# A transformer block in three-term fp32r: the two feed-forward stages start by token halves, with eight plain products in place of the first seven combined ones

## The reference, cut to what matters

```python
x = x + 0.5 * swiglu(rmsnorm(x, ffn1_norm), ffn1_w_gate, ffn1_w_up, ffn1_w_down)   # D_FF = 2816
h = rmsnorm(x, mix_norm)                                  # attention and RWKV-7 mixing on h @ w_in
...
x = x + merged @ w_out
x = x + memory_cross_attention(rmsnorm(x, cross_norm), rmsnorm(mem, mem_norm), w_cq, w_ckv, w_co)
x = x + 0.5 * swiglu(rmsnorm(x, ffn2_norm), ffn2_w_gate, ffn2_w_up, ffn2_w_down)
out = rmsnorm(x, final_norm)
# rmsnorm(x, g) = x * rsqrt(mean(x * x) + 1e-6) * g;  swiglu(h) = (silu(h @ gate) * (h @ up)) @ down
```

## Time and profile before

| | us |
|---|---|
| median of 3 runs (3218.71 to 3220.97) | 3220.22 |
| the profiled execution, its own time | 3219.02 |
| its span in the trace | 3217.2 |
| TensorE busy in it (91%) | 2943.0 |
| VectorE, GpSimd, ScalarE busy | 1621.0, 1353.7, 1087.4 |

### The profile page before, as it was taken

The page is one execution under the profiler, slowest core; times in us unless marked ns, Lnnn a source line. Parts: engine busy times, 40 slices in busy tenths (PEclk is TensorE's granted clock), DMA queues, the critical chain, the costliest instruction groups (busy, mean ns, idle before and its releaser), DMA issues. The chain is left out here.

```text
span 3217.2 us, 61692 instructions
## 1 busy us (share of the span) xinstructions
PE 2943.0 (91%) x26984; PEld 2412.2 (75%) x26984; DVE 1621.0 (50%) x1767; ACT 1087.4 (34%) x1780; POOL 1353.7 (42%) x705
## 2 busy tenths in 40 slices
PE   3799999996899999999999998899995799999995
PEld 2688888885677878778787887686774688887885
DVE  5654443445146666555666665243224645543445
ACT  2433333223234434334443333342212333333221
POOL 1344444443255555444555454462131344444441
PEclk7999999998999999999999999899997899999997
DMA  3222224442421211131121212351002222234441
GB/s 143 69 94 96 83 105 147 144 147 49 175 62 51 59 58 58 37 108 47 46 61 53 63 43 74 116 160 46 26 27 79 69 79 85 98 109 145 143 147 69
DMA packets 260169, 279.12 MB, mean 87 GB/s; under 512 B 13504, under 2 KB 213312, under 8 KB 257728
## 3 DMA queue, kind: packets, MB, share of 16 engines
q1 hardware_dynamic: 259904, 275.20, 26.2%
HBM read 224.83 MB, written 50.33 MB: 86 GB/s over the span
## 5 line engine op out<-in xcount | busy, mean ns | idle before, releaser
L483 POOL TENSOR_TENSOR w_low<-ffn_work,w_high 128x1024 fp32r<-128x1024 f32 x182 | 444.9, 2445 | 668.7 <-ACT w_high L556 395.4
L523 PE MATMUL bank<-h_high,w_high 128*128 128x512 f32 x1232 | 484.8, 393 | 59.1 <-DVE h_low L667 34.9
L523 PE MATMUL bank<-h_low,w_high 128*128 128x512 f32 x1232 | 483.4, 392 | 0.0
L523 PE MATMUL bank<-h_high,w_low 128*128 128x512 f32 x1232 | 483.4, 392 | 0.0
L1228 POOL TENSOR_TENSOR mix_panel_low<-arena,mix_panel_high 128x1024 fp32r<-128x1024 f32 x114 | 276.3, 2425 | 406.2 <-ACT mix_panel_high L1605 406.2
L1334 PE MATMUL bank<-mix_h_high,mix_panel_high 128*128 128x512 f32 (+1 forms) x896 | 357.7, 399 | 21.1 <-POOL mix_panel_low L1228 16.0
L1334 PE MATMUL bank<-mix_h_low,mix_panel_high 128*128 128x512 f32 (+1 forms) x896 | 342.0, 382 | 0.0
L1334 PE MATMUL bank<-mix_h_high,mix_panel_low 128*128 128x512 f32 (+1 forms) x896 | 340.7, 380 | 0.0
L714 DVE TENSOR_TENSOR h_low<-ffn_work,h_high 128x512 fp32r<-128x512 f32 x88 | 204.4, 2323 | 250.4 <-ACT h_high L571 250.4
L523 PEld LDWEIGHTS bank<-h_high,w_high 128*128 128x128 f32 x1232 | 234.1, 190 | 112.2 <-issue 61.4
L540 PE MATMUL bank<-h_high,w_high 128*128 128x512 f32 x704 | 274.8, 390 | 4.4 <-DVE h_low L714 4.4
(11 more groups left out here) (276 smaller groups left out, 5784.4 us busy)
## 6 DMA issues: line engine op xcount, KB each, us to landing
arena<-w_in SPq DMA_DIRECT2D x96, 512.0 KB, 3.8
ffn_work<-w_down SPq DMA_DIRECT2D x88, 512.0 KB, 3.6
a_spill<-ffn_work SPq DMA_DIRECT2D x88, 256.0 KB, 2.2
ffn_work<-a_spill SPq DMA_DIRECT2D x88, 256.0 KB, 2.6
ffn_work<-w_gate SPq DMA_DIRECT2D x12, 1024.0 KB, 5.7
ffn_work<-w_up SPq DMA_DIRECT2D x12, 1024.0 KB, 8.2
arena<-w_gate SPq DMA_DIRECT2D x10, 1024.0 KB, 5.6
arena<-w_up SPq DMA_DIRECT2D x10, 1024.0 KB, 8.2
```

The costliest lines, as they stand in the source:

```text
L483: nc.gpsimd.tensor_tensor(slot(w[1], q), src, slot(w[0], q).bitcast(F32), ALU.subtract).then_inc(s_low, 1)
L523: last = mm(bank[:, bk, :], w[wp][:, q % RING, kt, e], h[hp][:, k, kt], start=fresh and kt + wp + hp == 0, stop=kt == KT // 2 - 1 and wp = ...
```

## The change

Three parts go together.

**Start of the first feed-forward.** The block that loaded x is gone. x comes in 8 tiles of 128 tokens (`load_rows`), through three row buffers; ScalarE squares each tile in its buffer and sums the squares on the way (`accum_out`), TensorE turns it, VectorE (tiles 0 to 3) or ScalarE (4 to 7) puts it into `xT`. The norm runs over 512 tokens at a time.

**First group of both feed-forwards.** Eight plain products (`FIRST`) with five panels (`FIRST_PANELS`, one of them twice), those of token half 0 first; T1 to T4 are used from group 1 on.

**End of cross attention.** The closing projection makes panels 0 and 1 for both halves, then 2 to 7 for half 0, then 2 to 7 again for half 1, each with its own load, high and low part. The norm of half 0 for `ffn(1)` is made in between, its first weights are loaded and its first panel is split there. In `project_out` all low parts of panels go to VectorE; in the closing projection those of the first six units go to VectorE and the rest to GpSimd.

```diff
+        FIRST_PANELS = [A11, A12, A21, A22, A11]
+        FIRST = [(0, B11, C11, True), (1, B21, C11, False), (2, B11, C21, True), (3, B21, C21, False),
+                 (1, B22, C12, True), (3, B22, C22, True), (2, B12, C22, False), (4, B12, C12, False)]
```

SyncE in `ffn(0)` (`load_rows`; `keep_x(j)` waits until 256 tokens are placed and stores them, 1 MB), then in both:

```diff
+                        def tile(t):
+                            if t >= 3:
+                                sp.wait_ge(s_sq, t - 2)
+                            sp.dma_start(tiles[t % 3], d["x"][t * P:(t + 1) * P, :]).then_inc(s_tile[t % 3], 16)
...
+                        for t in range(3):
+                            tile(t)
+                        sp.dma_start(par[:], ...).then_inc(s_par, 16)
+                        first_weights(0)
+                        tile(3)
+                        keep_x(0)
+                        tile(4)
+                        keep_x(1)
+                        for t in range(5, 8):
+                            tile(t)
+                        first_weights(1)
+                        sp.dma_start(cst[:, n:], d["consts"][:, n:]).then_inc(s_rest, 16)
...
+                    keep_act(0, 0)
+                    keep_act(0, 2)
+                    sp.wait_ge(s_blow, low_at["T2"])
+                    sp.wait_ge(s_bsum, sums_before["T2"])
                     load_group(1)
```

GpSimd:

```diff
+                        nrm[0].pool_root(pool)
+                        subtract_low(0, block_of(0, FIRST_PANELS[0]))
...
+                    for q in range(1, NQ0):
+                        subtract_low(q, block_of(0, FIRST_PANELS[q]))
+                        if front and q == 1:
+                            nrm[1].pool_root(pool)
```

TensorE:

```diff
+                    if front:
+                        pe.wait_ge(s_ident, 16)
+                        for t in range(4):
+                            turn_tile(t)
+                        nrm[0].pe_scale(pe)
+                    else:
+                        nrm[1].pe_sums(pe)
+                    for r in range(len(FIRST)):
+                        first_product(r)
+                        if front and r < 2:
+                            turn_tile(4 + 2 * r)
+                            turn_tile(5 + 2 * r)
+                        elif front and r == 2:
+                            nrm[1].pe_scale(pe)
```

ScalarE:

```diff
+                    if front:
+                        for t in range(4):
+                            square_tile(t)
+                        round_first(0)
+                        nrm[0].act_high(act, range(0, 2))
+                        round_first(1)
+                        nrm[0].act_high(act, range(2, 6))
+                        place_tile(4)
+                        nrm[0].act_high(act, range(6, 8))
+                        place_tile(5)
+                        square_tile(4)
+                        square_tile(5)
+                        round_first(2)
+                        for t in (6, 7):
+                            place_tile(t)
+                        for t in (6, 7):
+                            square_tile(t)
+                    else:
+                        round_first(1)
+                        round_first(2)
+                    round_input("B22")
+                    round_first(3)
+                    round_input("B12")
+                    first_silu(0)
+                    round_input("T1")
+                    first_silu(2)
+                    round_input("T3")
+                    round_first(4)
+                    round_input("T2")
```

VectorE, behind the norm of half 1 with the scaling and low parts of B22 and B12:

```diff
+                    input_sum("T1", half_of(0, 0), half_of(0, 1), half_of(0, 0))
+                    input_sum("T3", half_of(0, 1), half_of(1, 1), half_of(0, 1))
+                    first_multiply(0)
+                    input_lows("T1")
+                    first_multiply(2)
+                    input_lows("T3")
+                    input_sum("T2", half_of(1, 1), half_of(1, 1), half_of(0, 0))
+                    input_lows("T2")
```

`cross`, SyncE (`keep_x` stores 1 MB each, once the given number of sums is there):

```diff
-                    for k in range(CO, CO + KT):
+                    for k in range(CO, CO + 4):
                         load(sp, k)
+                    sp.wait_ge(s_o, 2 * XH)
+                    for e, w in enumerate((panels(d["w_gate2"]), panels(d["w_up2"]))):
+                        sp.dma_start(ffn_raw[:, :, e], w[:, :, 0:2 * P]).then_inc(s_ffn, 16)
+                    for k in range(CO + 4, CO + KT + 2):
+                        load(sp, k)
+                    keep_x(0, 0, 10)
+                    keep_x(0, 1, 10)
+                    for k in range(CO + KT + 2, FFN_PANEL):
+                        load(sp, k)
+                    keep_x(1, 0, 12)
+                    keep_x(1, 1, 16)
```

`cross`, TensorE (`CLOSE` is 14):

```diff
+                    for u in range(2, CLOSE):
+                        panel_ready(pe, CO + u)
...
+                        out_part(u, 0, KT).then_inc(s_ready, 1)
+                        if u == KT:
+                            nf[0].pe_sums(pe)
+                        elif u == KT + 1:
+                            nf[0].pe_scale(pe)
```

`cross`, VectorE in `project_out`:

```diff
                         add_out(dve, n, o, k % 4, k + 1)
+                        subtract_low(dve, k % 2, k + 2, V)
```

783 lines of the change are left out of this document (458 added, 325 removed).

## The result

The changed kernel takes **3142.54 us** (median of 4 runs, 3142.12 to 3144.54) against 3220.59 before: a ratio of 0.976, 95% interval [0.975, 0.977], so 78 us less. Its profiled execution took 3142.14 us with a span of 3140.4, against 3219.02 and 3217.2 before: 76.9 us less. I had forecast 3143.

What follows compares the result with a forecast made beforehand. TensorE was 91% busy, its idle time mainly at both feed-forward starts, with group 0 bound by VectorE. Gains of 25.1 + 52 + 1 = 78.1 us took 3219.0 to 3140.9, median forecast 3143; 8 in 10: 3128 to 3162.

Steps and rivals of the forecast that it cites:

- First border: Start of first feed-forward up to group 1: group 1 starts at 103.5 instead of 128.6, 25.1 us gained; bounds 17 to 39.
- the 2 us that I charged VectorE: Price assumed in the forecast: VectorE loses 2 us for each panel low part that GpSimd makes beside it.
- the 112 that I gave: Sign in the first feed-forward: group 1's first addition at 112, from a start at 103.5 plus 8.2.
- The store of x: First border: scaling waits until 512 tokens of x are stored, at 21; 15.5 by the Trainium skill's rate.
- Squares with a sum on the way: Price of ScalarE's squaring with summing in the row tiles: taken as 1.1 us, at least 1.06, at most twice that.
- project_out: Low parts moved to VectorE fit its load and GpSimd's source low parts come earlier: 1 us gained; bounds -2 and +4.
- Closing projection and second border: Closing projection ends at 2445 against 2444.2; second feed-forward's group 1 starts at 2494 against 2547.6: 52 us gained, bounds 44 to 55.
- (a): Rival, first border: order of instructions does not bind; group 1 at 90 to 95, 10 us more gained, 3132; chance 0.13.
- (b): Rival, both groups 0: VectorE stays the bound, group 1 starts 8 later at each border, 3159; chance 0.13.
- (c): Rival, closing projection: stalls repeat in every unit, 12 units at 7.3 instead of 5.44, 22 us lost, 3165; chance 0.08.
- (d): Rival, groups after the borders: they lose their rhythm; gain gone at 3.9 us a group, 3243 at 5; chance 0.04.
- (e): Rival, both borders: nothing gained, idle time only moves behind the first products; 3218 to 3222; chance 0.02.

Runs made afterwards that it cites:

- e1: Changed kernel with, in the first border, ScalarE making panel 3's high part before the four of B22, not behind them; 3148.21 us, ratio 0.9766.
- e2: Changed kernel with, in the first border, GpSimd making panel 2's low part before the second half's root; 3137.52 us, ratio 0.9736.
- e3: Changed kernel with first border reordered: second half of first weights before tile 7, panels 2 and 3 split earlier, before the second root; 3133.04 us, ratio 0.9725.
- e8: Changed kernel with TensorE turning all eight row tiles before product 0 in the first border; 3142.44 us, ratio 0.9754.
- e6: Changed kernel with project_out's panel low parts back on GpSimd instead of VectorE; 3145.18 us, ratio 0.9758.
- e4: Changed kernel with the closing projection's load of panel 10 issued before the two stores of the first token half; 3140.82 us, ratio 0.9747.
- e5: Changed kernel with product 0 of the second border held until the second half's norm is turned and B22 scaled; 3154.93 us, ratio 0.979.
- e11: Changed kernel with all eight row tiles turned before product 0, plus weights before tile 7 and panel 2's low part before the second root; 3136.08 us, ratio 0.9734.

## Why the prediction was right, point by point

**The sum.** 78.1 us were forecast for the profiled execution and 76.9 came; 3143 for the median and 3142.5 came. The terms were less exact than the total: 27.9 us at the first border (25.1 forecast), 0.65 lost between the borders (1 gained forecast), 51.2 in the closing projection and the second border (52), and 1.7 lost at the end (0). That these errors nearly cancel is luck.

**First border, 25.1 forecast, 27.9 in the profile** and 24.4 to 27.9 over the six profiles with this front (174.87 less 146.9 to 150.4), so the term was right within what one execution can show. Its steps: first product near 24 (24.0); scaling from 21 (21.75, released by the store of x); squares to 52 (51.2); GpSimd's low part of A21 behind the root to 55.5 (54.8); product 3 after 9 us of idling at 72 (8.3 us, at 70.6); T2's sum done at 91 (87.2); load landed 99.4 (95.6). The one step that was mis-sized is the 2 us that I charged VectorE for each panel's low part beside it: up to T2's sum few of them met. Behind it more did (four low parts took 3.92 us for 2.50, the sum for T4 3.89 for 2.28), and group 1's first addition came 5 us later than the 112 that I gave. I had set TensorE's chain at 100.7 and the load's at 103.5; group 1 started at 100.3, the two together. e1, e2 and e3 bear out that both chains matter and that the lists set them. What the prediction did not see is e8: I had put down the gain to products that run while the second half is prepared ("68 and 42 us lie ahead of any product"), and in this border the early start itself was worth nothing. What e8 keeps and the kernel before had not are row tiles turned and squared as they land, half norms, and plain products in place of the first sums; which of them carries how much was not taken apart.

**The store of x.** I had worked the scaling's wait for it out as 21, from bytes that pass the queue at 0.34 MB/us, against 15.5 by the Trainium skill, "DMA: Bandwidth & Descriptors", section "Anatomy of one DMA — SWDGE (gpsimd) path". Measured: 21.75. That looks like a verdict on the rate and is none, for SyncE issued this store only at 15.74, when tile 3 had been placed, and it landed 6.0 us later. Neither sum counts from that issue. The rows are SyncE's issue and VectorE's first scaling in the changed kernel, then the stretch from 10 to 14 us of the kernel before, in which its queue moved x at 421 GB/s:

```profile
15.74 0.54 SPq L484 DMA_DIRECT2D x_spill<-arena  x1
```

```profile
21.75 1.40 DVE L285 SCALAR_TENSOR_TENSOR arena<-arena,bank 128x512 f32<-128x512 f32 x2 [1.62 <-DMA x_spill<-arena]
```

```profile
10.00:14.00 4.00, 0.00 (x0) 0.00 (x0) 0.00 (x0) 0.00 (x0) 0.00 (x0) 1.00 1.03 421
```

So my 0.34 MB/us was a misreading of the earlier trace rows (4.2 and 0.9 MB in 13 us are already 0.39), and "the 15.0 us of x speak against that rate" was wrong: x itself ran close to the 436 GB/s of the Trainium skill's fit. That 21 came out near 21.75 is luck.

**Squares with a sum on the way.** I wrote that they are not in the trace and took 1.1. That was a misreading: the kernel before has two such instructions at 806 us, in the norm of the memory rows (1.06 us each, with a read of the accumulator of 0.19). In the changed kernel one takes 1.04 to 1.08 us with a separate read of the accumulator of 0.19 to 0.22 beside it, so the 1.1 was near enough.

**project_out, 1 forecast, nothing found.** The additions span 85.99 us before, 85.92 after and 85.92 with the part undone (e6). The step that failed is "GpSimd's source low parts come earlier", which I took for 1 us: TensorE's wait for them was 0.6 us before, gone in the changed kernel and 0.5 again in e6, and the span of the stage did not follow. The 1.2 us that the ledger gains from project_out's first product to the closing projection are not shown to be the change's either: the way from the last of these additions to the first maximum of the heads was 40.1 us before and 37.9 in the changed profile, but 39.5 to 39.9 in seven of the twelve later ones.

**Closing projection and second border, 52 forecast together, 51.2 measured** (78.5 less 27.3). On TensorE the twelve single units took 69.1 us (2349.25 to 2418.3), where I had 69. The stall at panel 10 was foreseen at 2.5 us and its cause, the stores ahead of the load, was right (e4); it was 1.7 us. The gap at the block change is 4.0 us ("under 4"). Counted from the last closing addition, group 2's first addition came 54.2 us nearer (149.65 to 95.45 us) and group 1's 49, where I had 53 for group 1: as at the first border, group 1's first addition is late by VectorE's list. Product 0 starts at 2423.2, 3.3 us behind the last closing addition; e5 shows that here, other than at the first border, most or all of that start counts.

**The mixing stage, 0 to +1 forecast.** The profile shows 1.4 us lost between the first and the last scan, and the thirteen profiles span 4 us there. The copy of the table was not undone by itself, so a part of a microsecond stays open.

**The rivals.** (a), that the order of the lists does not bind, is refuted: the order was worth 9 to 13 us (e3), and with it mended group 1 started at 88.8 and the time was 3133, where (a) had 90 to 95 and 3132. (b), VectorE as the bound, is half true: in e3, with the lists mended, it is VectorE's sums and the load behind them that TensorE waits 11 us for. (c): one stall and not twelve. (d), the rhythm of the groups behind, is not touched: the changed kernel is 78.49 us ahead at group 2 of the second feed-forward and 78.49 at group 10 (2820.02 against 2898.51). (e): no.

## What to carry to other kernels

Two waits of 6 and 8 us stood side by side in one list of waits; one was worth all of its length and one nothing. Before removing a wait, look for what stands behind it in the waiting engine's own order: here the transpose on which the other engine's whole next stage hangs. And work that is started early is a gain only if the thing behind it can start early too: a head start of 21 us was worth nothing in one order of the other engines' lists (e8), and in the better order one of 16 to 17 us was worth 7 to 8 at the landmark (e11).

## What the runs showed of the hardware

**One stage, two durations.** With the same code of that stage (e5 left out), the way from the last closing addition to group 2 took 95.4 or 95.5 us in three profiles, 96.9 to 97.0 in seven and a value between in two, and the stretch of the four heads (first to last maximum) 120.6 or 120.7 in three, 123.8 to 124.1 in nine and 122.3 in one. The granted clock goes with it. From 15 us before the last closing addition to 25 behind it, in the changed kernel and in e4:

```profile
2404.93:2444.93 40.00, 35.99 (x157) 29.23 (x156) 34.07 (x40) 19.48 (x29) 13.33 (x7) 0.96 0.11 42
```

```profile
2403.84:2443.84 40.00, 35.99 (x150) 29.14 (x149) 32.48 (x39) 17.90 (x26) 13.31 (x7) 0.91 0.07 28
```

The same busy time holds 157 matmuls at 0.96 and 150 at 0.91. And the heads, in the changed kernel and in e1:

```profile
2191.53:2315.37 123.84, 117.00 (x481) 87.94 (x480) 35.45 (x21) 29.09 (x32) 24.08 (x14) 0.97 0.09 26
```

```profile
2198.91:2319.57 120.66, 113.81 (x481) 86.57 (x480) 35.44 (x21) 29.10 (x32) 24.09 (x14) 1.00 0.09 27
```

Both stages hold the same instructions in the two runs, and in all profiles but e5's the way to group 2 was 95.4 or 95.5 where the granted clock of that 40 us stretch was 0.96, and 96.1 or more where it was 0.91. So such steps of 1.6 and 3.2 us go with the clock and not with an edit: 3 us between two single profiles of this kernel prove nothing. The scatter of the mixing stage is another matter; its clock was 1.00 in runs of 1051.1 and of 1054.6 us, and what moves it was not found.

**GpSimd beside VectorE.** A spread copy of 512 columns on VectorE, begun 0.06 us behind a low part of GpSimd (52.46, 2.34 us), took 2.56 us in the changed kernel; in e3, with no low part beside it, 0.43:

```profile
52.52 2.56 DVE L278 COPY arena<-arena 128x512 f32<-128x512 f32 x1 [1.13 <-POOL arena L225]
```

```profile
48.16 0.43 DVE L278 COPY arena<-arena 128x512 f32<-128x512 f32 x1 [1.13 <-POOL arena L225]
```

In the changed kernel it ended 0.28 us behind the low part. The Trainium skill, "SBUF — State Buffer", section "Who interferes with whom", has it that the two engines share one port pair under an exclusive lock; the trace agrees.
